# The recurrent gates of a hybrid layer in four matmuls per channel tile instead of six, with high and low input stacked on the partition halves

## The chip, the cores and the metric

The kernel runs on one core of one Trainium2 chip. The metric is the device time in microseconds of one execution. The matmul engine is called PE, the vector engine DVE, the scalar engine ACT, GpSimd POOL; SP issues most DMAs.

## The reference, cut to what matters

Two layers over 1024 tokens of width 2048. Each has one combined projection of the normalised input; a sliding-window attention; and a recurrent part of 1024 channels, whose two gates (r and i) come from 16 blocks of 64 channels with 64x64 weights each. Everything is float32.

```python
for l in range(DEPTH):
    h = _rmsnorm(x, norm_gain[l])
    proj = jnp.einsum('bsd,de->bse', h, w_in[l])
    q, k, v, g_attn, x_rnn, g_rnn = jnp.split(proj, splits, axis=-1)
    attn = _swa_sink_attention(q, k, v, sinks[l], cos, sin)
    xc = _causal_conv(x_rnn, conv_w[l], conv_b[l])
    rnn = _rg_lru(xc, w_rgate[l], b_rgate[l], w_igate[l], b_igate[l], lru_param[l])
    mixed = jnp.concatenate([attn * jax.nn.silu(g_attn), rnn * jax.nn.silu(g_rnn)], axis=-1)
    x = x + jnp.einsum('bse,ed->bsd', mixed, w_out[l])
...
xb = xc.reshape(b, s, N_RNN_BLOCKS, RNN_BLOCK)
r = jax.nn.sigmoid(jnp.einsum('bshi,hij->bshj', xb, w_r).reshape(b, s, D_RNN) + b_r)
i = jax.nn.sigmoid(jnp.einsum('bshi,hij->bshj', xb, w_i).reshape(b, s, D_RNN) + b_i)
log_a = -LRU_C * r.astype(jnp.float32) * jax.nn.softplus(-lru_param.astype(jnp.float32))
a = jnp.exp(log_a)
mult = jnp.sqrt(-jnp.expm1(2.0 * log_a))
u = mult * (i * xc).astype(jnp.float32)
_, h = lax.associative_scan(_lin_combine, (a, u), axis=1)
```

## The kernel before

Tokens lie along the free dimension, channels on the 128 partitions. The sequence is done in two halves of 512 tokens (`h`), each through both layers (`l`), so a layer is passed four times. A pass is cut into 200 slots (`s`). In each slot PE does one unit of the large projections: 12 matmuls of 128x512 into `proj`, each tile's product being three matmuls, because a float32 operand is split into a high and a low part in a rounded format (`F32R`): high by high, high by low, low by high.

Every unit's weights (`wraw`) come by DMA four slots ahead; ACT rounds them to the high part (`weight_hi`, L471) and DVE subtracts for the low part (`weight_lo`, L774) three slots before PE needs them. ACT may round the weights of slot s + 3 only when PE has finished unit s - 1, so ACT's and DVE's work of slot s begins as PE begins unit s.

All other work is written by hand into these slots, and each engine runs its own instructions strictly in program order, with semaphores between the engines. Two lists place what matters here:

- The attention goes in 16 visits b at the slots `VISIT[b]` = 31, 35, 39, 44, 48, 53, 57, 61, 66, 70, 75, 79, 83, 88, 92, 97 (then 101, 105). PE does scores (L400), transposes of the probabilities (`prob_transposes`, L413, in slot `VISIT[b+1]+1`) and values (L421). The transposes of visit b wait until ACT has copied the result of visit b-1 out of the same PSUM bank (`attn_out`, L593, in the same slot of ACT's program). ACT's exponents are L577 and L579, its copy of the transposed probabilities L587.
- The recurrent channels go in 8 tiles j of 128 channels at the slots `R0[j]` = 48, 54, 64, 70, 80, 86, 96, 102. With S for `R0[j]`: in slot S DVE takes the projection out and starts the convolution (L922 to L936, done in S+1), ACT and DVE split the gate weights `gw` into `gwcut` (L602, L942). In S+2 ACT rounds the convolved tile `xc` (`conv_hi`, L609) and DVE subtracts (`conv_lo`, L948) into `xcut`. In S+3 PE computes the r gate of all 128 channels, in S+4 the i gate, each with three 128x512 matmuls (`gate`, L438) into the one PSUM bank `ps_g`; the 128x128 weights are two 64x64 blocks on the diagonal and zeros. ACT reads r out with a tanh in S+4 (`rnn_r`, L615) and i in S+5 (`rnn_i`, L622), into `r_in` and `i_in`, the two halves of `sqr`. Then follow `lru_z` on DVE (S+5), `rnn_a` on ACT (S+6), `lru_m2` (S+7), `rnn_mult` on ACT with a table load (L639, S+7), and in S+9 on DVE `lru_scan` (L969, L970), which reads `i_in`. `gate_tanh` (L569) belongs to the output gates.

Since `R0` advances by 6 slots from an even to an odd tile and by 10 from an odd to an even one, slot S+4 of an odd tile is the slot after the scan of the tile before.

Of the kernel before, what the change touches and what calls it, by code (L numbers as in the profile page):

```python
# [7 lines left out]
F32 = mybir.dt.float32  # L8
# [5 lines left out]
P = 128  # L14
# [5 lines left out]
HD = 64  # L20
# [78 lines left out]
def build(nc, xt, w, gates, par, fgain, cossin, ident, out):  # L99
    with ExitStack() as ctx:  # L100
# [26 lines left out]
        acc = sb("acc", [TOK])  # L127
        gw = sb("gw", [GRING, 2, HD])
        gwcut = sb("gwcut", [2, 2, P], F32R)
# [126 lines left out]
        def _(sp_):  # L256
# [17 lines left out]
            for h in range(HALVES):  # L274
                for l in range(DEPTH):
                    for s in range(SLOTS):
# [22 lines left out]
                        if s + 8 in R0:  # L299
                            j = R0.index(s + 8)  # L300
                            n = l * RT + j

                            sp_.wait_ge(gw_lo, h * (2 * DEPTH * RT) + (2 * n + 2))
                            sp_.dma_start(gw[:, n % GRING, :, :], gates[l, j]).then_inc(gw_in[n % GRING], 16)
# [12 lines left out]
        @block.gpsimd  # L317
        def _(pool):
            pool.memset(gwcut[:, :, :, :].bitcast(F32), 0.0).then_inc(pool_set, 1)
# [3 lines left out]
            pool.wait_ge(pool_set, 4)  # L323

        @block.tensor
        def _(pe):
# [28 lines left out]
            def sum_of_squares(h, n):  # L355

                pe.wait_ge(acc_done, at_acc(h, KT * (n + 1)))
                if h == 0 and n == 0:
                    pe.wait_ge(par_in, 32)
                    pe.wait_ge(pool_set, 4)  # L360
# [63 lines left out]

            def gate(h, l, j, which):

                n = l * RT + j
                if which == 0:
# [36 lines left out]
        def _(act):  # L465
# [192 lines left out]
            act.activation(sp[:, 1, :, :], sp[:, 0, :, :], ACT.Exp, scale=-1.0).then_inc(abs_done, 1)  # L658
            act.wait_ge(pool_set, 4)
            act.wait_ge(par_in, 32)  # L660
            for h in range(HALVES):
                for l in range(DEPTH):
                    for s in range(SLOTS):
# [41 lines left out]
                        if s - 4 in R0:  # L705
                            rnn_r(h, l, R0.index(s - 4))
                        if s - 1 in G0:
# [8 lines left out]
                        for j in range(RT):  # L716
                            if s == R0[j] + 7:
                                rnn_mult(h, l, j)
                            if s == R0[j]:
                                gate_weights_hi(h, l, j)  # L720
                            if s == R0[j] + 5:
                                rnn_i(h, l, j)
                            if s == R0[j] + 6:
                                rnn_a(h, l, j)
# [28 lines left out]
        def _(dve):  # L753
            dve.sem_inc(evac, 4)
            dve.sem_inc(q_done, 1)
            dve.sem_inc(gw_lo, 2 * GRING)
            dve.memset(eps[:, :], EPS).then_inc(dve_set, 1)
# [180 lines left out]
            def gate_weights_lo(h, l, j):  # L938
                n = l * RT + j
                dve.wait_ge(gw_hi, h * (2 * DEPTH * RT) + (2 * n + 2))  # L940
                for a in (0, HD):
                    dve.tensor_tensor(gwcut[a:a + HD, 1, :, a:a + HD], gw[a:a + HD, n % GRING, :, :],  # L942
                                      gwcut[a:a + HD, 0, :, a:a + HD].bitcast(F32),
                                      ALU.subtract).then_inc(gw_lo, 1)

            def conv_lo(h, l, j):
                dve.wait_ge(xc_hi, per_layer(h, l, RT, j + 1))
                dve.tensor_tensor(xcut[:, 1, :], xc[:, :], xcut[:, 0, :].bitcast(F32),  # L948
                                  ALU.subtract).then_inc(xc_lo, 1)

            def lru_z(h, l, j):

                dve.wait_ge(r_done, per_layer(h, l, RT, j + 1))
                dve.tensor_scalar(r_in, r_in, 1.0, decay4[:, l, j:j + 1], ALU.add, ALU.mult).then_inc(z_done, 1)

            def lru_input(h, l, j):

                dve.wait_ge(i_done, per_layer(h, l, RT, j + 1))
                mark(dve.scalar_tensor_tensor(i_in, i_in, 1.0, xc[:, :], ALU.add, ALU.mult))
# [49 lines left out]
            for u in (2, 3):  # L1009
                weight_lo(u)  # L1010
            dve.wait_ge(pool_set, 4)
            for h in range(HALVES):
# [139 lines left out]
```

## Time and profile before

| | |
|---|---|
| median of 3 runs | 2394.43 us (2394.32 to 2394.78) |
| profiled execution | 2394.46 us |
| span of its instructions | 2392.6 us |
| PE busy | 2361.0 us, 99% of the span |
| DVE busy | 1399.6 us, 58% |
| ACT busy | 1194.5 us, 50% |
| DMA engines busy | about 33% |
| PE's granted clock, mean | 0.997 |

The span runs from the first to the last instruction on the core; the profiled execution took 1.9 us more than its span, and lies with the other runs. Busy times say how long an engine worked in all, not whether its work was on the path that sets the end.

### The profile page before, as it was taken

How to read it: one execution, taken by the hardware profiler on the slowest of the kernel's cores; microseconds unless marked ns; L12 is line 12 of the kernel's file. 1: busy time of each engine (PE TensorE's matmuls, PEld its weight loads, DVE VectorE, ACT ScalarE, POOL GpSimd, SP SyncE). 2: the span in 40 equal slices, each digit the busy share in tenths (PEclk: the TensorE clock that was granted, in tenths of full speed). 3: DMA queues.
4: the chain of work that ended last, by engine and by line, in shares of the span. 5: the costliest groups of instructions: out<-in, count | busy, mean ns of one | idle time of the engine just before them, and what ended most of it. 6: DMA issues, size and time to landing. Idle time of an engine off the chain costs nothing. (4 is left out here: it accounts for less than half of the span.)

```text
span 2392.6 us, 31126 instructions
## 1 busy us (share of the span) xinstructions
PE 2361.0 (99%) x11380; PEld 1904.4 (80%) x11380; DVE 1399.6 (58%) x2447; ACT 1194.5 (50%) x2357; POOL 1.2 (0%) x8
## 2 busy tenths in 40 slices
PE   8999999999999999999999999999999999999996
PEld 6877778888887777888888777788888777788885
DVE  7567765534546776544476677654354567756334
ACT  6556663324455665434455666542244566654332
POOL 0000000000000000000000000000000000000000
PEclk9999999999999999999999999999999999999998
DMA  5324223333332222353334432333333322233332
GB/s 183 98 82 158 87 80 98 97 98 96 96 94 82 83 80 86 97 167 94 98 116 128 159 102 81 88 97 97 97 98 93 94 80 82 81 88 97 97 97 105
DMA packets 126297, 241.28 MB, mean 101 GB/s; under 512 B 14144, under 2 KB 18496, under 8 KB 125376
## 3 DMA queue, kind: packets, MB, share of 16 engines
q1 hardware_dynamic: 125136, 237.03, 32.7%
q8 instruction: 89, 1.46, 0.2%
q10 hardware_dynamic: 1008, 2.26, 0.2%
q14 instruction: 64, 0.52, 0.1%
HBM read 230.85 MB, written 8.39 MB: 100 GB/s over the span
## 5 line engine op out<-in xcount | busy, mean ns | idle before, releaser
L351 PE MATMUL proj<-operand,wcut 128*128 128x512 f32 x9600 | 2227.4, 391 | 7.7 <-DVE wcut L774 6.4
L351 PEld LDWEIGHTS proj<-operand,wcut 128*128 128x128 f32 x9600 | 1794.3, 188 | 393.0 <-issue 19.2
L774 DVE TENSOR_TENSOR wcut<-wraw,wcut 128x512 fp32r<-128x512 f32 x800 | 552.2, 690 | 911.8 <-ACT wcut L471 908.8
L471 ACT ACTIVATE wcut<-wraw 128x512 fp32r<-128x512 f32 x800 | 504.3, 630 | 986.8 <-PE proj L351 975.4
L579 ACT ACTIVATE prob<-ps_sc,stat 128x128 f32<-128x128 f32 x256 | 89.9, 368 | 0.1
L549 ACT ACTIVATE gy<-proj 32x512 f32<-32x512 f32 x144 | 84.9, 589 | 3.8
L511 ACT ACTIVATE sqr<-x 128x512 f32<-128x512 f32 x64 | 38.0, 635 | 56.7 <-DVE x L979 56.6
L438 PE MATMUL ps_g<-xcut,gwcut 128*128 128x512 f32 x192 | 57.5, 408 | 0.0
L803 DVE TENSOR_TENSOR acc<-acc,sqr 128x512 f32<-128x512 f32 x78 | 53.9, 691 | 4.7
L639 ACT ACT_TABLE_LOAD x32 | 41.1, 1283 | 27.4 <-DVE mu L964 27.1
L579 ACT ACTIVATION_READ_ACCUMULATOR prob<-ps_sc,stat 128x1 f32 x256 | 53.4, 209 | 0.0
L934 DVE SCALAR_TENSOR_TENSOR xc<-xr,pars,xc 128x512 f32<-128x512 f32 x64 | 48.1, 752 | 2.1
L979 DVE TENSOR_TENSOR x<-proj,x 128x512 f32<-128x512 f32 x64 | 41.2, 685 | 11.6 <-PE proj L351 10.7
L569 ACT ACTIVATE gt<-gy 128x512 f32<-128x512 f32 x64 | 40.4, 632 | 14.2 <-DVE gy L883 12.7
L400 PEld LDWEIGHTS ps_sc<-kboth,q 64*64 64x64 f32 x1024 | 27.2, 132 | 24.4 <-issue 24.4
L915 DVE TENSOR_TENSOR prob<-prob,stat 128x512 f32<-128x512 f32 x64 | 44.3, 692 | 2.2
L895 DVE TENSOR_TENSOR mixed<-mixed,gy 128x512 f32<-128x512 f32 x64 | 44.3, 692 | 2.1
L905 DVE TENSOR_REDUCE stat<-ps_sc 128x4 f32<-128x512 f32 x64 | 44.2, 690 | 2.0
L878 DVE TENSOR_TENSOR gy<-proj,rstd 128x512 f32<-128x512 f32 x64 | 44.2, 690 | 1.9
L785 DVE TENSOR_TENSOR operand<-mixed,operand 128x512 fp32r<-128x512 f32 x64 | 41.7, 688 | 5.3 <-ACT operand L493 4.5
L883 DVE SCALAR_TENSOR_TENSOR gy<-gt,gy 128x512 f32<-128x512 f32 x64 | 43.9, 685 | 0.8
L413 PE MATMUL ps_t<-idn,prob 128*128 128x128 f32 x256 | 38.5, 273 | 4.8 <-ACT mixed L593 4.8
(108 smaller groups left out, 1100.7 us busy)
## 6 DMA issues: line engine op xcount, KB each, us to landing
wraw<-in_w SPq DMA_DIRECT2D x800, 256.0 KB, 2.6
x<-in_xt SPq DMA_DIRECT2D x2, 4096.0 KB, 13.3
mixed<-in_xt SPq DMA_DIRECT2D x14, 512.0 KB, 8.4
out<-x SPq DMA_DIRECT2D x4, 1024.0 KB, 4.7
tab<-in_cossin SPq DMA_DIRECT2D x8, 256.0 KB, 3.4
gw<-in_gates SPq DMA_DIRECT2D x32, 64.0 KB, 2.5
out<-x ACTq DMA_DIRECT2D x4, 512.0 KB, 2.9
out<-x SPq DMA_DIRECT2D x3, 512.0 KB, 2.9
```

What stands on the lines that cost most here:

```text
L351: last = pe.matmul(bank[:, :], wcut[:, u % RING, a, c:c + P], operand[:, k, b, :], start=(k == 0 and n == 0), stop=(k == KT - 1 and n == 2))
L438: last = pe.matmul(ps_g[:, :], gwcut[:, a, which, :], xcut[:, b, :], start=i == 0, stop=i == 2)
L471: act.activation(wcut[:, u % RING, 0, :], wraw[:, u % RING, :], ACT.Copy).then_inc(w_hi, 1)
L549: act.activation(gy[dst:dst + 32, 1, :], bank_of(l, tile)[src:src + 32, :], ACT.Copy).then_inc(shift_done, 1)
L579: act.activation(prob[:, t, :], ps_s[:, t // 2, t % 2, :], ACT.Exp, scale=HD ** -0.5, bias=stat[:, 1, t:t + 1], accum_out=stat[:, 3, t:t + ...
L774: dve.tensor_tensor(wcut[:, u % RING, 1, :], wraw[:, u % RING, :], wcut[:, u % RING, 0, :].bitcast(F32), ALU.subtract).then_inc(w_lo, 1)
L803: ins = dve.tensor_tensor(acc[:, :], acc[:, :], sqr[:, k % 2, :], ALU.add)
L878: dve.tensor_tensor(gy[:, n % 2, :], bank_of(l, tile)[:, :], rstd[:, :], ALU.mult).then_inc(evac, 1)
L895: dve.tensor_tensor(mixed[:, k, :], mixed[:, k, :], gy[:, n % 2, :], ALU.mult).then_inc(mixed_done, 1)
L905: mark(dve.tensor_reduce(stat[:, 0, :].rearrange("p (o a) -> p o a", o=2), ps_s, AX_X, ALU.max))
L915: dve.tensor_tensor(prob[:, :, :], prob[:, :, :], stat[:, 3, :].unsqueeze(2).to_broadcast([P, TPK, P]), ALU.mult).then_inc(p_done, 1)
L934: mark(dve.scalar_tensor_tensor(xc[:, :], src, wc, xc[:, :], ALU.mult, ALU.add))
```

## The change

The product of one tile is arranged anew. The unit is now one block of 64 channels (`part` 0 or 1) with both its gates, where it was one gate of both blocks. The contraction over 128 partitions holds the high part of the block's 64 inputs on one half and their low part on the other; the weights, repeated on both halves, hold r's and i's 64 columns side by side. So one matmul gives the high weights times high and low input, a second the low weights times both: two matmuls per block, four per tile.

```diff
-        gw = sb("gw", [GRING, 2, HD])
+        gw = sb("gw", [GRING, 2, P])
...
-            def gate(h, l, j, which):
+            def gate(h, l, j, part):
...
-                    pe.wait_ge(xc_lo, per_layer(h, l, RT, j + 1))
-                    pe.wait_ge(gw_lo, h * (2 * DEPTH * RT) + (2 * n + 2 + 2 * GRING))
+                    pe.wait_ge(xc_lo, per_layer(h, l, 2 * RT, 2 * j + 2))
+                    pe.wait_ge(gw_lo, h * (DEPTH * RT) + (n + 1 + GRING))
                     if j > 0:
-                        pe.wait_ge(i_done, per_layer(h, l, RT, j))
+                        pe.wait_ge(i_done, per_layer(h, l, 2 * RT, 2 * j))
                 else:
-                    pe.wait_ge(r_done, per_layer(h, l, RT, j + 1))
-                for i, (a, b) in enumerate(((0, 0), (0, 1), (1, 0))):
-                    last = pe.matmul(ps_g[:, :], gwcut[:, a, which, :], xcut[:, b, :],
-                                     start=i == 0, stop=i == 2)
+                    pe.wait_ge(i_done, per_layer(h, l, 2 * RT, 2 * j + 1))
+                for a in range(2):
+                    last = pe.matmul(ps_g[:, :], gwcut[:, part, a, :], xcut[:, part, :], start=a == 0, stop=a == 1)
...
-                for a in (0, HD):
-                    act.activation(gwcut[a:a + HD, 0, :, a:a + HD], gw[a:a + HD, n % GRING, :, :],
-                                   ACT.Copy).then_inc(gw_hi, 1)
+                act.activation(gwcut[:, :, 0, :], gw[:, n % GRING, :, :], ACT.Copy).then_inc(gw_hi, 1)
...
-                act.activation(xcut[:, 0, :], xc[:, :], ACT.Copy).then_inc(xc_hi, 1)
-            def rnn_r(h, l, j):
-                act.wait_ge(g_done, per_layer(h, l, 2 * RT, 2 * j + 1) + 2 * GRING)
-                if j > 0:
+                for part in range(2):
+                    rows = slice(HD * part, HD * part + HD)
+                    act.activation(xcut[rows, part, :], xc[rows, :], ACT.Copy).then_inc(xc_hi, 1)
+            def gate_out(h, l, j, part):
+                act.wait_ge(g_done, per_layer(h, l, 2 * RT, 2 * j + part + 1) + 2 * GRING)
+                if j > 0 and part == 0:
                     act.wait_ge(m2_done, per_layer(h, l, RT, j))
-                act.activation(r_in, ps_g[:, :], ACT.Tanh, scale=0.5,
-                               bias=pars[:, l, C_BR + j:C_BR + j + 1]).then_inc(r_done, 1)
-            def rnn_i(h, l, j):
-                act.wait_ge(g_done, per_layer(h, l, 2 * RT, 2 * j + 2) + 2 * GRING)
-                if j > 0:
                     act.wait_ge(scan_done, per_layer(h, l, RT, j))
-                act.activation(i_in, ps_g[:, :], ACT.Tanh, scale=0.5,
-                               bias=pars[:, l, C_BI + j:C_BI + j + 1]).then_inc(i_done, 1)
+                a, b = HD * part, HD * (1 - part)
+                act.activation(r_in[a:a + HD, :], ps_g[a:a + HD, :], ACT.Tanh, scale=0.5,
+                               bias=pars[a:a + HD, l, C_BR + j:C_BR + j + 1]).then_inc(r_done, 1)
+                act.activation(i_in[a:a + HD, :], ps_g[b:b + HD, :], ACT.Tanh, scale=0.5,
+                               bias=pars[b:b + HD, l, C_BI + j:C_BI + j + 1]).then_inc(i_done, 1)
...
             def conv_lo(h, l, j):
-                dve.wait_ge(xc_hi, per_layer(h, l, RT, j + 1))
-                dve.tensor_tensor(xcut[:, 1, :], xc[:, :], xcut[:, 0, :].bitcast(F32),
-                                  ALU.subtract).then_inc(xc_lo, 1)
+                for part in range(2):
+                    a, b = HD * part, HD * (1 - part)
+                    dve.wait_ge(xc_hi, per_layer(h, l, 2 * RT, 2 * j + part + 1))
+                    dve.tensor_tensor(xcut[b:b + HD, part, :], xc[a:a + HD, :],
+                                      xcut[a:a + HD, part, :].bitcast(F32), ALU.subtract).then_inc(xc_lo, 1)
...
-                dve.wait_ge(r_done, per_layer(h, l, RT, j + 1))
+                dve.wait_ge(r_done, per_layer(h, l, 2 * RT, 2 * j + 2))
```

The slots stay as they were: `gate_out(.., 0)` stands where `rnn_r` stood (S+4), `gate_out(.., 1)` where `rnn_i` stood (S+5). DVE's split of the gate weights becomes one operation over 128 partitions instead of two over 64, the gates' DMA carries 128 KB instead of 64 KB, and one memset at the start is gone. The rest of the diff renumbers waits and lays out weights and biases on the host.

On ACT, around tile 3 of a pass, from the rounding of its input to its gates' read-out, this stood before (names in brackets are the semaphores waited for; the numbers behind `w_in` are buffers):

```order
L609 ACTIVATE xcut<-xc 128x512 [waits g_done,conv_done,w_hi]
L587 ACTIVATE probT<-ps_t 128x512 [waits v_done,t_done]
L577 ACT_TABLE_LOAD [waits t_done]
L577 ACTIVATE stat<-stat 128x4 [waits max_done]
L579 ACTIVATE prob,stat<-ps_sc,stat 128x128 x4
L471 ACTIVATE wcut<-wraw 128x512 [waits unit_done,w_in0]
L569 ACTIVATE gt<-gy 128x512 [waits gate_done,evac,w_hi]
L471 ACTIVATE wcut<-wraw 128x512 [waits unit_done,w_in1]
L615 ACTIVATE sqr<-ps_g,pars 128x512 [waits m2_done,g_done,w_hi]
L471 ACTIVATE wcut<-wraw 128x512 [waits unit_done,w_in2]
L569 ACTIVATE gt<-gy 128x512 [waits gate_done,evac,w_hi]
L622 ACTIVATE sqr<-ps_g,pars 128x512 [waits scan_done,g_done]
```

and this stands there now, from the same place on (lines are those of the changed kernel):

```order
L607 ACTIVATE xcut<-xc 64x512 [waits g_done,conv_done,w_hi]
L607 ACTIVATE xcut<-xc 64x512
L585 ACTIVATE probT<-ps_t 128x512 [waits v_done,t_done]
...
L469 ACTIVATE wcut<-wraw 128x512 [waits unit_done,w_in1]
L616 ACTIVATE sqr<-ps_g,pars 64x512 [waits m2_done,scan_done,g_done,w_hi]
L618 ACTIVATE sqr<-ps_g,pars 64x512
L469 ACTIVATE wcut<-wraw 128x512 [waits unit_done,w_in2]
L567 ACTIVATE gt<-gy 128x512 [waits gate_done,evac,w_hi]
L616 ACTIVATE sqr<-ps_g,pars 64x512 [waits g_done]
L618 ACTIVATE sqr<-ps_g,pars 64x512
```

Each single operation on 128 partitions has become two on 64, and the wait for the scan (`scan_done`) has moved from the second read-out to the first, one slot earlier.

On PE, at the same tile, before:

```order
L438 MATMUL ps_g<-xcut,gwcut 128x512 [waits i_done,gw_lo,xc_lo]
L438 MATMUL ps_g<-xcut,gwcut 128x512 x2
L351 MATMUL proj<-operand,wcut 128x512 [waits w_lo]
L351 MATMUL proj<-operand,wcut 128x512 x11
L438 MATMUL ps_g<-xcut,gwcut 128x512 [waits r_done]
L438 MATMUL ps_g<-xcut,gwcut 128x512 x2
```

and now:

```order
L437 MATMUL ps_g<-xcut,gwcut 128x512 [waits i_done,gw_lo,xc_lo]
L437 MATMUL ps_g<-xcut,gwcut 128x512
L350 MATMUL proj<-operand,wcut 128x512 [waits w_lo]
L350 MATMUL proj<-operand,wcut 128x512 x11
L437 MATMUL ps_g<-xcut,gwcut 128x512 [waits i_done]
L437 MATMUL ps_g<-xcut,gwcut 128x512
```

One matmul is gone from each group, and the second group, which waited for the r read-out, waits for both read-outs of the first block; one unit of 12 matmuls still lies between the groups.

## Rows read from the trace of the kernel before

**Rows 1.** Windows of the whole run: PE busy (count), granted clock; first column the stretch

```profile
6.40:10.40 4.00, 4.00 (x10) 3.13 (x11) 2.46 (x4) 2.62 (x6) 0.00 (x0) 1.00 1.02 378
40.00:2370.00 2330.00, 2324.31 (x11237) 1876.17 (x11237) 1358.27 (x2384) 1161.74 (x2303) 0.00 (x0) 1.00 0.33 98
2373.00:2379.20 6.20, 1.98 (x4) 0.67 (x4) 3.40 (x2) 3.91 (x6) 0.00 (x0) 1.00 0.00 0
2379.30:2392.60 13.30, 0.00 (x0) 0.00 (x0) 9.57 (x16) 0.00 (x0) 0.00 (x0) 0.50 0.80 315
```

**Rows 2.** Timeline, PE, the first tile's gates: start us, length us, operation

```profile
162.21 0.85 PE L438 MATMUL ps_g<-xcut,gwcut 128*128 128x512 f32 x3
...
162.90 2.91 PE L351 MATMUL proj<-operand,wcut 128*128 128x512 f32 x12
```

**Rows 3.** Groups by shape, whole run: busy us, mean ns of one

```profile
L615 ACT ACTIVATE sqr<-ps_g,pars 128x512 f32<-128x512 f32 x32 | 22.1, 689 | 17.9 <-PE ps_g L438 11.3 <-issue 4.2 <-ACT wcut L471 2.0
...
L609 ACT ACTIVATE xcut<-xc 128x512 fp32r<-128x512 f32 x32 | 20.3, 633 | 30.2 <-DVE xc L936 25.6 <-ACT wcut L471 2.9 <-issue 1.3
...
L942 DVE TENSOR_TENSOR gwcut<-gw,gwcut 64x128 fp32r<-64x128 f32 x64 | 18.2, 284 | 1.4
```

**Rows 4.** Timeline, tile 3 of the second layer, first half

```profile
821.72 0.63 ACT L609 ACTIVATE xcut<-xc 128x512 fp32r<-128x512 f32 x1 [0.98 <-ACT wcut L471]
822.26 0.58 ACT L587 ACTIVATE probT<-ps_t 128x512 f32<-128x512 f32 x1
...
826.30 0.69 DVE L774 TENSOR_TENSOR wcut<-wraw,wcut 128x512 fp32r<-128x512 f32 x1 [2.74 <-ACT wcut L471]
...
827.49 0.69 ACT L615 ACTIVATE sqr<-ps_g,pars 128x512 f32<-128x512 f32 x1
...
828.56 0.85 PE L438 MATMUL ps_g<-xcut,gwcut 128*128 128x512 f32 x3
828.77 1.28 DVE L970 TENSOR_TENSOR_SCAN mixed<-acc,hlast,sqr 128x512 f32<-128x512 f32 x1
```

**Rows 5.** Timeline, tile 1 of the same layer

```profile
772.54 1.28 DVE L970 TENSOR_TENSOR_SCAN mixed<-acc,hlast,sqr 128x512 f32<-128x512 f32 x1
...
774.20 0.37 ACT L593 ACTIVATE mixed<-ps_t 128x256 f32<-128x256 f32 x1
...
776.10 0.60 PE L413 MATMUL ps_t<-idn,prob 128*128 128x128 f32 x4
...
780.98 0.69 DVE L774 TENSOR_TENSOR wcut<-wraw,wcut 128x512 fp32r<-128x512 f32 x1 [2.00 <-ACT wcut L471]
...
788.01 0.39 ACT L593 ACTIVATE mixed<-ps_t 128x256 f32<-128x256 f32 x1
...
789.55 0.60 PE L413 MATMUL ps_t<-idn,prob 128*128 128x128 f32 x4
```

**Rows 6.** Timeline, tiles 4 and 5 of the same layer

```profile
866.48 0.63 ACT L471 ACTIVATE wcut<-wraw 128x512 fp32r<-128x512 f32 x1 [0.53 <-PE proj L351]
...
877.29 1.28 ACT L569 ACT_TABLE_LOAD   x1 [0.33 <-issue]
...
879.12 0.36 ACT L593 ACTIVATE mixed<-ps_t 128x256 f32<-128x256 f32 x1
...
879.63 0.63 PE L413 MATMUL ps_t<-idn,prob 128*128 128x128 f32 x4 [0.95 <-ACT mixed L593]
...
880.38 1.28 DVE L970 TENSOR_TENSOR_SCAN mixed<-acc,hlast,sqr 128x512 f32<-128x512 f32 x1
...
883.53 0.85 PE L438 MATMUL ps_g<-xcut,gwcut 128*128 128x512 f32 x3
```

**Rows 7.** Timeline, tile 6 of the same layer

```profile
908.68 0.63 ACT L609 ACTIVATE xcut<-xc 128x512 fp32r<-128x512 f32 x1 [2.59 <-DVE xc L936]
909.22 0.36 ACT L593 ACTIVATE mixed<-ps_t 128x256 f32<-128x256 f32 x1
...
909.73 0.63 PE L413 MATMUL ps_t<-idn,prob 128*128 128x128 f32 x4 [0.24 <-ACT mixed L593]
```

More of the change, by code:

```diff
@@ L301, in _ @@
                             n = l * RT + j
-                            sp_.wait_ge(gw_lo, h * (2 * DEPTH * RT) + (2 * n + 2))
+                            sp_.wait_ge(gw_lo, h * (DEPTH * RT) + (n + 1))
                             sp_.dma_start(gw[:, n % GRING, :, :], gates[l, j]).then_inc(gw_in[n % GRING], 16)
@@ L318, in _ @@
         def _(pool):
-            pool.memset(gwcut[:, :, :, :].bitcast(F32), 0.0).then_inc(pool_set, 1)
             pool.memset(ones[:, :], 1.0).then_inc(pool_set, 1)
@@ L322, in _ @@
             pool.memset(vhist[:, :, :], 0.0).then_inc(pool_set, 1)
-            pool.wait_ge(pool_set, 4)
+            pool.wait_ge(pool_set, 3)
         @block.tensor
@@ L359, in sum_of_squares @@
                     pe.wait_ge(par_in, 32)
-                    pe.wait_ge(pool_set, 4)
+                    pe.wait_ge(pool_set, 3)
                 if n:
@@ L423, in values @@
                 last.then_inc(v_done, 1)
-            def gate(h, l, j, which):
+            def gate(h, l, j, part):
                 n = l * RT + j
-                if which == 0:
-                    pe.wait_ge(xc_lo, per_layer(h, l, RT, j + 1))
-                    pe.wait_ge(gw_lo, h * (2 * DEPTH * RT) + (2 * n + 2 + 2 * GRING))
+                if part == 0:
+                    pe.wait_ge(xc_lo, per_layer(h, l, 2 * RT, 2 * j + 2))
+                    pe.wait_ge(gw_lo, h * (DEPTH * RT) + (n + 1 + GRING))
                     if j > 0:
-                        pe.wait_ge(i_done, per_layer(h, l, RT, j))
+                        pe.wait_ge(i_done, per_layer(h, l, 2 * RT, 2 * j))
                 else:
-                    pe.wait_ge(r_done, per_layer(h, l, RT, j + 1))
-                for i, (a, b) in enumerate(((0, 0), (0, 1), (1, 0))):
-                    last = pe.matmul(ps_g[:, :], gwcut[:, a, which, :], xcut[:, b, :],
-                                     start=i == 0, stop=i == 2)
+                    pe.wait_ge(i_done, per_layer(h, l, 2 * RT, 2 * j + 1))
+                for a in range(2):
+                    last = pe.matmul(ps_g[:, :], gwcut[:, part, a, :], xcut[:, part, :], start=a == 0, stop=a == 1)
                 last.then_inc(g_done, 1)
@@ L658, in _ @@
             act.activation(sp[:, 1, :, :], sp[:, 0, :, :], ACT.Exp, scale=-1.0).then_inc(abs_done, 1)
-            act.wait_ge(pool_set, 4)
+            act.wait_ge(pool_set, 3)
             act.wait_ge(par_in, 32)
@@ L705, in _ @@
                         if s - 4 in R0:
-                            rnn_r(h, l, R0.index(s - 4))
+                            gate_out(h, l, R0.index(s - 4), 0)
                         if s - 1 in G0:
@@ L721, in _ @@
                             if s == R0[j] + 5:
-                                rnn_i(h, l, j)
+                                gate_out(h, l, j, 1)
                             if s == R0[j] + 6:
@@ L755, in _ @@
             dve.sem_inc(q_done, 1)
-            dve.sem_inc(gw_lo, 2 * GRING)
+            dve.sem_inc(gw_lo, GRING)
             dve.memset(eps[:, :], EPS).then_inc(dve_set, 1)
@@ L939, in gate_weights_lo @@
                 n = l * RT + j
[L940 to L944, printed above, removed]
-            def conv_lo(h, l, j):
-                dve.wait_ge(xc_hi, per_layer(h, l, RT, j + 1))
-                dve.tensor_tensor(xcut[:, 1, :], xc[:, :], xcut[:, 0, :].bitcast(F32),
-                                  ALU.subtract).then_inc(xc_lo, 1)
+                dve.wait_ge(gw_hi, h * (DEPTH * RT) + (n + 1))
+                dve.tensor_tensor(gwcut[:, :, 1, :], gw[:, n % GRING, :, :], gwcut[:, :, 0, :].bitcast(F32),
+                                  ALU.subtract).then_inc(gw_lo, 1)
+            def conv_lo(h, l, j):
+                for part in range(2):
[3 more added lines that the diff above has]
+                                      xcut[a:a + HD, part, :].bitcast(F32), ALU.subtract).then_inc(xc_lo, 1)
             def lru_z(h, l, j):
-                dve.wait_ge(r_done, per_layer(h, l, RT, j + 1))
+                dve.wait_ge(r_done, per_layer(h, l, 2 * RT, 2 * j + 2))
                 dve.tensor_scalar(r_in, r_in, 1.0, decay4[:, l, j:j + 1], ALU.add, ALU.mult).then_inc(z_done, 1)
             def lru_input(h, l, j):
-                dve.wait_ge(i_done, per_layer(h, l, RT, j + 1))
+                dve.wait_ge(i_done, per_layer(h, l, 2 * RT, 2 * j + 2))
                 mark(dve.scalar_tensor_tensor(i_in, i_in, 1.0, xc[:, :], ALU.add, ALU.mult))
@@ L1010, in _ @@
                 weight_lo(u)
-            dve.wait_ge(pool_set, 4)
+            dve.wait_ge(pool_set, 3)
             for h in range(HALVES):
@@ L1129 @@
     wo = arr(w_out).reshape(DEPTH, UPG, KU, P, OG, GW).transpose(0, 4, 1, 3, 2, 5)
-    first = {"q": 0, "kv": 4, "ga": 5, "xr": 9, "gr": 13, "o": PG}
-    source = [first[GROUPS[g][0]] + GROUPS[g][1] for g, _ in STREAM]
+    start = {"q": 0, "kv": 4, "ga": 5, "xr": 9, "gr": 13, "o": PG}
+    source = [start[GROUPS[g][0]] + GROUPS[g][1] for g, _ in STREAM]
     w = np.concatenate([wi, wo], axis=1)[:, source, [j for _, j in STREAM]]
     w = w.reshape(DEPTH, SLOTS, P, KU * GW)
-    gates = np.stack([arr(w_rgate), arr(w_igate)], axis=3).reshape(DEPTH, RT, P, 2, HD)
+    wr, wg = (arr(a).reshape(DEPTH, RT, 2, HD, HD) for a in (w_rgate, w_igate))
+    first = np.concatenate([wr[:, :, 0], wg[:, :, 0]], axis=3)
+    second = np.concatenate([wg[:, :, 1], wr[:, :, 1]], axis=3)
+    gates = np.tile(np.stack([first, second], axis=3), (1, 1, 2, 1, 1))
     sink = arr(sinks).reshape(DEPTH, NKV, 2, 2, 2).transpose(3, 0, 1, 4, 2).reshape(2, DEPTH, AT)
@@ L1138 @@
     cw = tiles(conv_w).transpose(0, 1, 3, 2).reshape(P, DEPTH, RT * CW)
-    par = np.concatenate([tiles(norm_gain), sink, cw, tiles(conv_b), tiles(b_rgate), tiles(b_igate),
+    bi = np.roll(tiles(b_igate), HD, axis=0)
+    par = np.concatenate([tiles(norm_gain), sink, cw, tiles(conv_b), tiles(b_rgate), bi,
                           tiles(lru_param)], axis=2)
```

## The prediction

> **What bounds the kernel now.** I read the windows first: between 40 and 2370 us PE is busy 2324.31 of 2330.00 us at the full granted clock, DVE and ACT about half the time [rows 1]. So PE's queue sets the time: a matmul removed counts in full, and so does every wait inserted. Then I read the timeline around the gates for the price of one matmul: three begin at 162.21 and the unit behind them at 162.90, so one takes 0.23 us [rows 2], not the 0.85 that the row shows from first start to last end. Last I went, tile by tile, to the instruction that releases PE behind each gate, to see how much earlier than PE it was ready. That is the reading that decides here: ACT and DVE have room on average, but each runs in order, and PE's waits on them sit at a few fixed places.
>
> **What the change removes.** 2 of 6 matmuls in each of 32 tiles: 64 x 0.23 = 14.7 us, 3.68 us for each of the four passes through a layer. PE has nothing else to do then, so all of it counts if nothing else is late. The new matmuls have the same shape and should cost the same. The memset and the larger gates DMA cost nothing: the memset's engine is idle, and the weights are asked for eight slots ahead of their use.
>
> **What it adds.** No row shows these operations on 64 partitions. Below, a half-width operation could cost half; above, as much as the full one: 633 ns for the rounding, 689 for the tanh [rows 3]. The nearest row is DVE's split of the gate weights on 64 partitions, 284 ns for 128 elements a partition [rows 3]: 0.41 of the tanh's time for a quarter of its length, which is no sign of a discount for half the partitions. I take the full durations. Two in a row overlap a little: from one start to the next 0.54 us on ACT [rows 4], and about 0.59 for the tanh. So ACT gets 0.54 in S+2 and 0.59 in each of S+4 and S+5; DVE gets 0.6 for the second subtraction, and saves some 0.17 on the gate weights (two operations of 284 against one of twice the row length; between 0 and 0.3). That is 55 us more work on ACT in all, hidden behind PE's units except where PE is released by it. Four places are left.
>
> *Tile 3.* This is the large term. The first read-out now writes half of `i_in` too, so it waits for the scan of tile 2, which reads `i_in`. In the trace the r read-out began at 827.49, and that scan ran from 828.77 to 830.05 [rows 4]. The chain that leads to the scan starts at the rounding at 821.72; the second rounding puts 0.54 in front of the exponents, DVE waits 2.74 us for what follows them (826.30), and 0.17 is saved before: the scan ends 0.37 later, at 830.42. Then 0.04 to start, 0.59 + 0.69 for the two tanh, and 0.15 until PE goes on (an ACT result at 879.48 released PE at 879.63 [rows 6]): 831.89. PE arrives at its second group at 828.56 less the matmul saved in the first, 828.33. It stands for **3.56 us**. Queued behind are unit 75 and all of PE's program, so it counts in full. Bounds: with roundings and tanh at half price 2.7, with no overlap and nothing saved on DVE 3.9. The other three passes have the same order.
>
> *Tile 1.* The scan of tile 0 ended at 773.82 [rows 5]; the second subtraction stands right before it on DVE, so 774.42. The two tanh take ACT to 775.64, and behind them in its queue is `attn_out` (0.37 us), for which PE's transposes wait: 776.01 + 0.15 = 776.16, where PE would be at 776.10 - 0.23 = 775.87. That is 0.29. In the next slots DVE's delay of 0.6 passes to ACT and the second block's extra tanh adds 0.59; DVE was already waiting 2.00 us for ACT at 780.98 [rows 5], so all of it, some 1.15, reaches the `attn_out` that ended at 788.40. PE's transposes then start at 789.70, with PE there at 789.55 - 0.46 + 0.29 = 789.38: 0.32. Together **0.61**; bounds 0 and 1.2.
>
> *Tiles 4 and 5.* Before tile 5's gates PE already waits 0.95 us for ACT [rows 6]. What is saved on tile 4 (0.46) only lengthens that wait, unless ACT is early too. ACT had 0.53 of idle time at 866.48 for the extra tanh, which leaves its chain some 0.2 early; the second rounding adds 0.54, against 0.33 idle at 877.29. The transposes then start where they did: the 0.46 is lost. The scan of tile 4 ends at 881.66 - 0.2 + 0.6 = 882.06, so PE is released at 882.06 + 0.04 + 0.59 + 0.69 + 0.15 = 883.53, and would be there at 883.30: 0.23. Together **0.69**; bounds 0.3 and 1.3.
>
> *Tile 6.* PE waits 0.24 for `attn_out`, which follows the rounding directly [rows 7]. The second rounding, less the 0.17, delays it by **0.37**; bounds 0 and 0.6.
>
> Elsewhere the read-outs end a microsecond or more before PE needs them.
>
> **The sum.** Per pass: -3.68 + 3.56 + 0.61 + 0.69 + 0.37 = +1.55. Four passes: +6.2 us. The profiled execution took 2394.46 us, 0.03 off the median, so 2394.46 + 6.2 = **2400.7 us**. The bounds of the four places add up to 3.0 and 7.0 a pass, which gives 4 x (-3.68 + 3.0) = -2.7 to 4 x (-3.68 + 7.0) = +13.3: 2391.7 to 2407.7. The likeliest case's own range is 2397 to 2405.
>
> **Rivals.**
> - *The clock falls in the waits.* At the end of the run PE's last work ended at about 2375, the granted clock was still 1.00 until 2379.2, and 0.50 after 2379.3 [rows 1]. [...] If it falls, the units behind run slow until the clock is given back. At the start of the run PE's first 4.00 us held 10 matmuls [rows 1], where 17 fit at 0.23: 1.7 us lost. Four falls: 2400.7 + 6.8 = 2407.5, more if the clock stays low longer. Against it: the wait is shorter than the one that is known to have dropped it. [...]
> - *Only the large wait is real.* The small ones rest on sums of tenths. If slack swallows them, each pass is -3.68 + 3.56: 2394.0, no change. For it: most of them are 0.2 to 0.4 us. Against: at 879.63 and 909.73 PE waits for ACT already, and there any delay counts.
> - *The saving wins.* The scan of tile 2 comes early enough. It decides from a wait of about 2.4 us: with 0.9 us less in front of the scan, or half-width tanh and roundings much cheaper than full ones. If tile 3 had but its second tanh to wait for (r ended 0.38 before PE's 828.56 [rows 4]), its wait would be 0.2 to 0.4, and the sum -3.68 + 0.3 + 1.67 = -1.7 a pass: 2387.6; with no waits at all 2379.8. Against: `scan_done` is waited for by name, and its time is read from the trace.
>
> **How the numbers follow.** A difference of 0.2%, 4.8 us, is about what a measurement of this kernel can tell from no change. I give the forecast 0.47, the clock 0.18, only the large wait 0.24, the saving 0.11. Slower by over 0.2% means above 2399.2: about two thirds of the forecast's 2397 to 2405 and all of the clock's, with a tail of the forecast's beyond.  Slower 0.54, within 0.2% 0.35, faster 0.11. The range goes from the lower bound of the sum (2392) to the clock's case with something over (2409), which leaves out the saving's 2387.6 and below.
>
> **What would show it.** Right: ps_g's matmuls number 128 and are 0.23 apart; in the list of PE's waits a new row, second gate group on ACT's tanh, four times 3.3 to 3.9 us and four times about 0.2; the transposes (L413 before) wait more than 4.8 us in all, some 9; the first read-out of tile 3 starts 0.05 after the scan's end; ACT's 64-partition tanh lasts about 690 ns; the granted clock stays at 1.00 between first and last unit. Wrong: a half-width tanh near 350 ns; the scan of tile 2 ending before PE's first group; waits of PE for weights (`wcut`), since ACT stands blocked for some 3 us at tile 3 with the rounding of unit 78's weights behind it (four slots of room, so I cost it at nothing; gone, it would cost the excess over 8 us); or a clock of 0.50 behind a wait.

## The result, and the profile after

The changed kernel takes 2421.73 us (median of four runs, 2420.25 to 2423.5) against 2394.59 beside it (2394.32 to 2394.78): 27.1 us more, ratio 1.0114, interval 1.0098 to 1.013. The predicted time was 2400.7. Direction and largest term came out, the size did not. The profiled execution took 2422.28 us, 27.8 more than that of before.

The page of the changed kernel (busy, share of the span, count; then groups: busy, mean ns of one | idle before, releaser):

```profile
PE 2361.0 (98%) x11316; PEld 1899.2 (78%) x11316; DVE 1418.2 (59%) x2447; ACT 1258.5 (52%) x2421; POOL 0.7 (0%) x7
...
L616 ACT ACTIVATE sqr<-ps_g,pars 64x512 f32<-64x512 f32 x64 | 43.8, 684 | 36.4 <-DVE mixed L966 27.0 <-PE ps_g L437 8.2
L437 PE MATMUL ps_g<-xcut,gwcut 128*128 128x512 f32 x128 | 44.8, 432 | 15.2 <-ACT sqr L618 15.2
...
L607 ACT ACTIVATE xcut<-xc 64x512 fp32r<-64x512 f32 x64 | 40.4, 631 | 27.1 <-DVE xc L932 23.1
...
L944 DVE TENSOR_TENSOR xcut<-xc,xcut 64x512 fp32r<-64x512 f32 x64 | 43.9, 686 | 2.8 <-ACT xcut L607 0.9
```

Half the partitions bring no discount at all: the tanh takes 684 ns on 64 partitions against 689 on 128, the rounding 631 against 633 [rows 3]. PE's busy time stands at 2361.0 as before, although 64 matmuls are gone. That is the first sign that some of its matmuls ran slower. The waits show how long PE stood (total us, times, longest):

```profile
PE ps_t L412 <- ACT mixed L591: 18.0, 16, 2.0
PE ps_g L437 <- ACT sqr L618: 15.2, 7, 3.6
PE proj L350 <- DVE wcut L770: 6.5, 1, 6.5
```

The second row is the forecast's new wait, four times 3.6 us and three times 0.23. The first was forecast at some 9 us and is twice that. The third, at the start of the run, was there before.

The timeline of tile 3, second layer, first half (start us, length us), answers to [rows 4]:

```profile
831.91 0.62 PE L437 MATMUL ps_g<-xcut,gwcut 128*128 128x512 f32 x2
...
832.37 2.92 PE L350 MATMUL proj<-operand,wcut 128*128 128x512 f32 x12
...
836.06 1.28 DVE L966 TENSOR_TENSOR_SCAN mixed<-acc,hlast,sqr 128x512 f32<-128x512 f32 x1
...
837.46 0.68 ACT L616 ACTIVATE sqr<-ps_g,pars 64x512 f32<-64x512 f32 x1 [2.71 <-DVE mixed L966]
...
838.17 0.68 ACT L618 ACTIVATE sqr<-ps_g,pars 64x512 f32<-64x512 f32 x1
...
838.91 1.22 PE L437 MATMUL ps_g<-xcut,gwcut 128*128 128x512 f32 x2 [3.62 <-ACT sqr L618]
```

The first read-out stands until the scan of tile 2 is done, then the two tanh start 0.71 us apart, and PE follows. Unforecast are the 1.22 us of the last row: the same two matmuls took 0.62 at 831.91. The windows of the low clock, between the first and the last unit, say why (stretch, its length, PE busy and count; behind the other engines the granted clock, then DMA share and GB/s; last their sum). The granted clock reads 0.50 in each of them, and 1.00 in all other time between those two units:

```profile
244.41:247.82 3.41, 3.41 (x10) 2.53 (x8) 1.05 (x2) 1.36 (x2) 0.00 (x0) 0.50 0.38 115
838.33:841.74 3.41, 2.83 (x7) 2.25 (x8) 2.91 (x5) 3.15 (x5) 0.00 (x0) 0.50 0.27 77
892.94:896.36 3.42, 3.42 (x10) 2.67 (x9) 3.31 (x6) 1.90 (x3) 0.00 (x0) 0.50 0.12 40
1435.66:1442.49 6.83, 5.33 (x13) 4.17 (x14) 3.79 (x7) 3.99 (x6) 0.00 (x0) 0.50 0.33 98
2032.99:2039.82 6.83, 5.99 (x14) 4.46 (x14) 3.14 (x6) 3.39 (x6) 0.00 (x0) 0.50 0.33 96
sum 23.90, PE 20.98 PEld 16.09 DVE 14.21 ACT 13.79 POOL 0.00; mean PE 4.20 PEld 3.22 DVE 2.84 ACT 2.76 POOL 0.00
```

Four of the five go with tile 3's wait, one in each pass; 892.94 follows a wait of 1.98 us before tile 5's gates. At 838.33, 1435.66 and 2032.99 it fell while PE still stood; at 244.41 and 892.94 it fell 1.3 and 1.2 us after PE had gone on. In all, PE worked 21.0 us at a granted clock of 0.50. The pair's 1.22 us against 0.62 put work there at twice its time, so the cost is estimated at up to half of the 21.0.

### The profile page after: what moved, and what is told of

It reads as the page before. It is cut to its first block and busy times, and to the rows that moved or that the text cites. A ratio compares the mean times of both kernels' runs of the same rounds, so it can differ in the third digit from the quotient of the medians.

```text
span 2420.5 us, 31069 instructions
## 1 busy us (share of the span) xinstructions
PE 2361.0 (98%) x11316; PEld 1899.2 (78%) x11316; DVE 1418.2 (59%) x2447; ACT 1258.5 (52%) x2421; POOL 0.7 (0%) x7
## 5 line engine op out<-in xcount | busy, mean ns | idle before, releaser
L616 ACT ACTIVATE sqr<-ps_g,pars 64x512 f32<-64x512 f32 x64 | 43.8, 684 | 36.4 <-DVE mixed L966 27.0
L437 PE MATMUL ps_g<-xcut,gwcut 128*128 128x512 f32 x128 | 44.8, 432 | 15.2 <-ACT sqr L618 15.2
L607 ACT ACTIVATE xcut<-xc 64x512 fp32r<-64x512 f32 x64 | 40.4, 631 | 27.1 <-DVE xc L932 23.1
L412 PEld LDWEIGHTS ps_t<-idn,prob 128*128 128x128 f32 x256 | 30.5, 139 | 30.5 <-issue 24.3
L944 DVE TENSOR_TENSOR xcut<-xc,xcut 64x512 fp32r<-64x512 f32 x64 | 43.9, 686 | 2.8 <-ACT xcut L607 0.9
## 6 DMA issues: line engine op xcount, KB each, us to landing
x<-in_xt SPq DMA_DIRECT2D x2, 4096.0 KB, 13.6
```

What stands on the lines that cost most here:

```text
L412: last = pe.transpose(ps_t[:, t, :], prob[:, t, :], idn[:, :])
L437: last = pe.matmul(ps_g[:, :], gwcut[:, part, a, :], xcut[:, part, :], start=a == 0, stop=a == 1)
```

## The experiments

Three questions: what the large wait costs and whether the clock belongs to it; why the small waits are twice what was forecast; and what the four matmuls are worth without the waits. "Before" and "changed" name the kernel an edit was made in. All times stand beside 2394.5 to 2394.6 for the kernel before.

### The scan's wait alone, in before

```diff
+                    act.wait_ge(scan_done, per_layer(h, l, RT, j))   # in rnn_r
...
-                    act.wait_ge(scan_done, per_layer(h, l, RT, j))   # in rnn_i
```

> The kernel before, with nothing moved but the wait for the scan: it stands at the r read-out (slot S+4) instead of the i read-out (S+5). Theory (a wait counts in full, and the clock falls only in a longer stand): at tile 3 the r read-out starts after 830.05 instead of at 827.49, so PE's second gate group starts at 830.05 + 0.04 + 0.69 + 0.15 = 830.93 instead of 828.56: 2.37 us a pass, 9.5 us in all, about 2404 us; tiles 1 and 5 have room for it; clock at 1.00 throughout. Rival (any stand of a few us drops the clock): the same waits and low-clock stretches behind them, 1.7 to 3.4 us more for each, 2411 to 2418 us. Rival (the wait is hidden): 2395 us.

2408.1 us, ratio 1.0056 (1.0039 to 1.0073). Its waits, PE's timeline at tile 3, and windows behind it:

```profile
PE ps_g L438 <- ACT sqr L616: 8.8, 4, 2.2
```

```profile
829.37 2.90 PE L351 MATMUL proj<-operand,wcut 128*128 128x512 f32 x12
834.47 0.97 PE L438 MATMUL ps_g<-xcut,gwcut 128*128 128x512 f32 x3 [2.20 <-ACT sqr L616]
835.28 4.51 PE L351 MATMUL proj<-operand,wcut 128*128 128x512 f32 x12
```

```profile
835.32:838.73 3.41, 3.41 (x10) 2.64 (x9) 2.18 (x4) 1.21 (x2) 0.00 (x0) 0.50 0.49 106
838.75:842.00 3.25, 3.25 (x30) 2.06 (x29) 1.39 (x3) 2.06 (x5) 0.00 (x0) 1.00 0.21 73
```

A unit that lasts 2.90 us before the wait lasts 4.51 behind it. By the units' start times the wait costs 2.47 us a pass, 9.9 in all; the remaining 3.7 are the clock's. It fell behind three of the four waits, though each was the same 2.2 us. So both theories hold half: the wait as worked out, and the clock on top.

### Only the halves, in before

Rounding, subtraction and both read-outs each as two operations on 64 partitions; matmuls and waits as before. Shown for the rounding, the rest likewise:

```diff
-                act.activation(xcut[:, 0, :], xc[:, :], ACT.Copy).then_inc(xc_hi, 1)
+                for a in (0, HD):
+                    act.activation(xcut[a:a + HD, 0, :], xc[a:a + HD, :], ACT.Copy).then_inc(xc_hi, 1)
```

> The kernel before, with its six matmuls and their order, but the rounding, the subtraction and both read-outs of a tile done in two operations of 64 partitions each instead of one of 128. Theory (two operations on different partition halves do not overlap at all, so a pair costs 0.66 more on ACT for the rounding and 0.71 for a tanh, and the delay is handed on from tile 5 to tile 6): PE waits 1.1 at tile 3, 0.5 more at tile 5's transposes, some 1.3 more at tile 6's: 2.9 a pass, 11.7 in all, about 2406 us. Rival (they overlap as the prediction had it, 0.54 and 0.59, and nothing is handed on): 0.75 + 0.2 + 0.54 a pass, about 2400.6 us. Rival (half as many partitions take half the time): 2395 us.

2408.74 us, ratio 1.0059 (1.0044 to 1.0074).

```profile
PE ps_t L413 <- ACT mixed L593: 13.2, 12, 1.8
...
PE ps_g L438 <- ACT sqr L617: 4.1, 4, 1.0
```

The small waits come from the halves alone, and they are larger than forecast even without the large wait: +14.2 us. By the units' start times in the third pass they cost 0.69 us at tile 1, 1.28 at tile 3, 0.81 at tile 5 and 0.79 at tile 6. The theory's 1.3 at tile 6 did not come: DVE lies 10.4 us later than before there, and so does PE, so nothing is handed on. No clock is in this number:

```profile
40.00:2385.00 2345.00, 2326.82 (x11241) 1876.32 (x11240) 1381.29 (x2417) 1231.66 (x2400) 0.00 (x0) 1.00 0.33 97
```

### The halves, one kind at a time, in before

First the rounding and the subtraction alone, then the read-outs alone, with the edit above cut to these.

> The kernel before, with only the rounding and the subtraction of a tile's input in two operations of 64 partitions; read-outs and matmuls as before. Theory (a pair does not overlap: 0.66 on ACT): PE waits 0.43 at tile 3, 0.33 more at tile 5's transposes, 0.66 more at tile 6's: 1.4 a pass, about 2400.2 us. Rival (what costs is the read-outs): 2396 us or less.

> The kernel before, with only the two read-outs in two operations of 64 partitions each; rounding, subtraction and matmuls as before. Theory (0.71 more in S+4 and in S+5, handed on along ACT's and DVE's queues): 0.5 at tile 3, 0.2 at tile 5's transposes, 0.7 handed on to tile 6's, 0.3 at tile 1's second transposes: 1.7 a pass, about 2401 us; tile 6's transposes wait longer though nothing in front of them changed since the end of tile 5. Rival (tile 6's wait comes from its own rounding alone, nothing is handed on): 0.24 there as before, 2398.5 us.

2402.01 us (ratio 1.0031, 1.0019 to 1.0043) and 2398.1 us (ratio 1.0015, 1.0005 to 1.0024). PE's waits, first kernel:

```profile
PE ps_t L413 <- ACT mixed L593: 10.1, 8, 1.7
...
PE ps_g L438 <- ACT sqr L616: 1.3, 4, 0.3
```

and second:

```profile
PE ps_t L413 <- ACT mixed L593: 6.1, 8, 1.3
PE ps_g L438 <- ACT sqr L616: 0.9, 4, 0.2
```

The roundings cost 7.5 us, the read-outs 3.5: together 11.0, where both at once cost 14.2. So 3.2 us exist only together. In the second kernel tile 6's wait stayed at 0.24, which fits the rival of its expectation: alone, the read-outs of tile 5 hand nothing on to tile 6. Both at once leave 0.53 at tile 1's later transposes, which neither does alone; most of the 3.2 us are there (0.69 a pass by start times), the rest at tile 3.

### Two matmuls per gate, in before

The third product of each gate is left out, so the gates lack it; nothing else changes.

```diff
-                for i, (a, b) in enumerate(((0, 0), (0, 1), (1, 0))):
+                for i, (a, b) in enumerate(((0, 0), (0, 1))):
```

> The kernel before, with the third matmul of each gate (low weights by high input) left out, so the gates are computed from the high part of the weights alone. Everything else is as before. It measures the saving of 64 matmuls by itself. Theory: 64 x 0.23 = 14.7 us less, of which some 1 us is lost at tile 5's transposes, where PE waits for ACT anyway: about 2381 us. Rival (the saving is smaller than its share of PE's time, since PE's other waits swallow it): 2388 us or more.

2380.86 us, ratio 0.9943 (0.9928 to 0.9958). 13.65 us for 64 matmuls are 0.213 each, not 0.23. The waits at the transposes stayed at 0.95 and 0.24, and the saving counted all the same. That the theory's 2381 was met is luck: it took a larger saving less 1 us of loss, and there was no loss. The prediction's step that what is saved on tile 4 only lengthens tile 5's wait does not hold here: ACT's chain starts from PE's units and came as much earlier.

### The large wait filled, in the changed kernel

Thirteen matmuls of zero weights go into the bank of the unit in progress ahead of the wait at tile 3; they add nothing to its sum. The zeros are set once at the start.

```diff
+                    if j == 3:
+                        g = STREAM[R0[j] + 4][0]
+                        bank = proj[2 * ((l * (PG + OG) + g) % 2)]
+                        for _ in range(FILL):
+                            pe.matmul(bank[:, :], zero[:, :], operand[:, 0, 0, :], start=False, stop=False)
```

> The changed kernel, with 13 idle matmuls ahead of the wait at tile 3's second gate group: zero weights, accumulated into the bank in progress, so that they add nothing to the result. They fill 13 x 0.23 = 3.0 of the 3.8 us in which PE stands there, and take nothing away from the wait itself. Theory (part of the loss is the clock that falls behind this wait): the gap shrinks to some 0.8 us, the second group starts when it did, no low-clock stretch at tile 3, and the time falls by the clock's share of the loss, some 8.7 us by the low-clock stretches of the changed kernel: about 2413 us. Rival (the low clock in the record costs nothing, the waits are longer than counted): 2421 us, or more if the filling itself costs.

2414.38 us, ratio 1.0083 (1.0068 to 1.0098): 7.35 us under the changed kernel. PE's timeline, and windows before and behind the gate:

```profile
834.66 3.20 PE L442 MATMUL proj<-operand,zero 128*128 128x512 f32 x13
838.44 0.73 PE L445 MATMUL ps_g<-xcut,gwcut 128*128 128x512 f32 x2 [0.58 <-ACT sqr L626]
839.01 2.90 PE L353 MATMUL proj<-operand,wcut 128*128 128x512 f32 x12
```

```profile
834.70:838.40 3.70, 3.16 (x14) 2.22 (x12) 3.60 (x7) 1.37 (x2) 0.00 (x0) 1.00 0.25 71
838.44:842.00 3.56, 3.56 (x16) 2.71 (x18) 2.33 (x4) 2.60 (x4) 0.00 (x0) 1.00 0.40 97
1486.91:1490.32 3.41, 3.41 (x11) 2.83 (x12) 3.24 (x8) 1.13 (x3) 0.00 (x0) 0.50 0.24 77
```

From the unit ahead to the gate it is 6.54 us in both kernels (831.90 to 838.44; 832.37 to 838.91 in the changed kernel), so the gate was ready no sooner; but its two matmuls take 0.73 instead of 1.22 and the unit behind 2.90. The 7.35 us are therefore clock, and a lower bound for its price at tile 3: the third window is one of two falls that came behind the 1.98 us before tile 5, where the changed kernel has one.

### A buffer of its own for i of odd tiles, in the changed kernel

The read-out of tile j then waits for the scan of tile j-2.

```diff
+        def i_of(j):
+            return vfeat[:, 0:TOK] if j % 2 else i_in
...
-                    act.wait_ge(scan_done, per_layer(h, l, RT, j))
+                if j > 1 and part == 0:
+                    act.wait_ge(scan_done, per_layer(h, l, RT, j - 1))
```

> The changed kernel, with the i gate of odd tiles in a buffer that is free at that time, so that a tile's first read-out waits for the scan of the tile two before it, and never in fact. Nothing else differs. Theory (the wait for the scan makes PE stand long enough for the clock to fall): the scan's part of tile 3's wait goes, 1.4 of 3.8 us is left because ACT comes late; the first wait at tile 1 and the gate's at tile 5 go; no low-clock stretch; the waits that are left, about 3.7 us a pass, eat the saving of 3.68: about 2395 us. Rival (the loss is in the half-width operations and not in the wait for the scan): over 2410 us. Rival (the clock falls whatever the wait): low-clock stretches remain, over 2403 us.

2400.95 us, ratio 1.0026 (1.0015 to 1.0037): 20.8 us under the changed kernel, and 6 over what was expected.

```profile
PE ps_t L415 <- ACT mixed L594: 15.6, 12, 2.0
...
PE ps_g L440 <- ACT vfeat L622: 3.7, 4, 0.9
```

```profile
1505.98 0.63 PE L415 MATMUL ps_t<-idn,prob 128*128 128x128 f32 x4 [0.76 <-ACT mixed L594]
```

The large wait is down to 0.9, but the small ones keep 15.6 us, and behind two of the four waits of 1.97 to 1.98 us the clock fell. Of the 15.6, 4.8 stood there before the change; the other 10.8 and the 3.7 at tile 3 together outweigh the saving of 13.65. The last row is tile 6's wait in the third pass: 0.76, where the changed kernel has 1.75.

### Second block's work in other slots as well

On top of the kernel above, the second block's rounding and subtraction move to S+3, behind `attn_out`, and its read-out to the front of ACT's slot S+5. PE's first group then waits for the first block's subtraction alone.

```diff
+                        if s - 5 in R0:
+                            gate_out(h, l, R0.index(s - 5), 1)
...
+                        if s - 3 in R0:
+                            conv_hi(h, l, R0.index(s - 3), 1)
```

> The changed kernel with the i gate of odd tiles in its own buffer, and two things moved: the second block's rounding and subtraction one slot later (S+3, behind the copy of the attention's result), the second read-out to the front of slot S+5, ahead of the exponents. Theory (what is left of the loss is ACT's order at three places): tile 3 still waits about 1, tile 1's second transposes none, tile 5's 1.0 as before the change, tile 6's about 0.3; the rest of the saving of 13.6 comes through: about 2386 us, clock at 1.00 throughout. Rival (ACT and DVE simply have too much to do in these slots, so the waits only move): 2395 us or more.

2392.12 us, ratio 0.999 (0.9981 to 0.9999), 6 over what was expected.

```profile
PE ps_t L415 <- ACT mixed L595: 10.0, 8, 1.6
...
PE ps_g L441 <- ACT vfeat L622: 4.1, 4, 1.0
```

The second rounding no longer stands before `attn_out`, yet the transposes still wait, 0.89 at tile 1 and 1.6 at tile 5. What else stands ahead of `attn_out` in ACT's slot is the next suspect.

### The attention copy at the front of ACT's slot

Twice: on top of the last kernel (with tile 1's `rnn_mult` one slot later, and tile 3's first read-out ahead of `weight_hi`), and alone in before.

```diff
+                        for b in range(NB):
+                            if s == VISIT[b + 2] + 1:
+                                attn_out(h, l, b)
```

> The version with its own i buffer and the moved slots, and three more things moved on ACT: the copy of the attention's result (for which PE's transposes wait) to the front of its slot, tile 1's root with its table load one slot later, and tile 3's first read-out ahead of the rounding of weights in its slot. Theory (all of the loss was the order of ACT's work in front of three waits of PE, not its amount): the transposes wait for nothing, also not the 0.95 and 0.24 of before the change; tile 3 waits some 0.5 at most; the 13.6 us of the saving and the 6 of the old waits come through: about 2377 us. Rival (the amount of ACT's work binds in these slots): no better than 2388 us.

> The kernel before, with the copy of the attention's result at the front of its slot on ACT, and nothing else changed. It says how much of the last version's time has nothing to do with the gates. Theory: the eight waits of PE's transposes (0.95 and 0.24 in each pass, 1.1 and 0.4 by the start times) go: 6 us less, about 2388.5 us. Rival (they only move to the read-outs behind the copy): 2393 us or more.

2379.79 us (2379.56 to 2380.08), ratio 0.9939 (0.9925 to 0.9952), and 2388.26 us, ratio 0.9973 (0.9963 to 0.9983). In both the transposes wait for nothing. All that is left of the changed gates' waits in the first, and its window:

```profile
PE ps_g L441 <- ACT vfeat L622: 3.5, 8, 0.5
```

```profile
40.00:2360.00 2320.00, 2314.87 (x11184) 1866.02 (x11182) 1377.47 (x2386) 1225.07 (x2370) 0.00 (x0) 1.00 0.34 99
```

Between the two lies the worth of the four matmuls once ACT's order suits them: 2388.26 - 2379.79 = 8.5 us. The 13.65 of the matmuls less the 3.5 of waits would be 10.2. Most of the difference is that a wait costs more than its row says: by start times, against the second kernel, PE loses 0.52 us at tile 3's second gate group and 0.70 at tile 5's in each pass, 4.9 in all, which leaves 8.8. The last 0.3 us are not accounted for.

## Why the prediction was wrong

**PE as the bound, and the saving.** Right. Every wait and every matmul counted in full; a matmul is worth 0.213 us, which makes the saving 13.65 instead of 14.7.

**Durations of the halves.** Right: full price, 684 and 631 ns; DVE's split of the gate weights takes 0.42 where two took 0.57 [rows 3].

**Tile 3.** Right in place, mechanism and nearly in size: by start times 3.78 us a pass against 3.56. The scan's wait alone gives 2.47 there (first experiment), the halves alone 1.28 (second).

**Spacing of the halves.** The first step that failed: the overlap of [rows 4], 0.54 from one start to the next, was carried to pairs that start on different partition halves. The timeline of the changed kernel at tile 1:

```profile
774.39 1.29 ACT L607 ACTIVATE xcut<-xc 64x512 fp32r<-64x512 f32 x2
...
776.85 1.40 DVE L944 TENSOR_TENSOR xcut<-xc,xcut 64x512 fp32r<-64x512 f32 x2
```

Two roundings of 0.63 take 1.29, two subtractions of 0.69 take 1.40: no overlap. The tanh pair starts 0.71 apart. The operation behind a pair does not overlap either: in the third pass the next rounding of weights starts 1.32 us after the pair's first (1486.90 and 1488.22), where it started 0.54 after the single rounding before the change. So to what stands behind it a second rounding costs 0.77 instead of 0.54, a second tanh 0.84 instead of 0.59, a second subtraction 0.84 instead of 0.6. On DVE too the next subtraction (`weight_lo`) starts 1.43 us after the pair's first in the third pass (1488.36 and 1489.79), where it started 0.60 after the single one before (1469.14 and 1469.74). What decides it was tried on neither engine.

**The small waits.** Terms of the sum mis-sized, by the units' start times in the third pass, in us a pass:

| place | predicted | measured |
|---|---|---|
| tile 1 | 0.61 | 1.45 |
| tile 3 | 3.56 | 3.78 |
| tiles 4 and 5 | 0.69 | 1.55 |
| tile 6 | 0.37 | 1.50 |

With the saving at 3.68, as the terms were read with 0.23 a matmul, this is +4.60 instead of +1.55; with all four passes like the third, +18.4 instead of +6.2. Tile 6 shows the kind of error that weighs most. It was taken as fed afresh by PE, so that only its own second rounding counted. ACT and then PE in the third pass of the changed kernel:

```profile
1493.83 0.69 ACT L616 ACTIVATE sqr<-ps_g,pars 64x512 f32<-64x512 f32 x1 [2.25 <-DVE mixed L966]
...
1506.20 0.63 ACT L635 ACTIVATE mu<-mu 128x512 f32<-128x512 f32 x1 [1.37 <-DVE mu L960]
...
1517.07 0.63 ACT L469 ACTIVATE wcut<-wraw 128x512 fp32r<-128x512 f32 x1 [2.11 <-PE proj L350]
1521.01 1.28 ACT L607 ACTIVATE xcut<-xc 64x512 fp32r<-64x512 f32 x2 [3.31 <-DVE xc L932]
1522.32 0.39 ACT L591 ACTIVATE mixed<-ps_t 128x256 f32<-128x256 f32 x1
```

```profile
1518.06 3.04 PE L350 MATMUL proj<-operand,wcut 128*128 128x512 f32 x12
1522.84 0.63 PE L412 MATMUL ps_t<-idn,prob 128*128 128x128 f32 x4 [1.75 <-ACT mixed L591]
```

DVE's convolution of tile 6, in before and in the changed kernel:

```profile
1499.86 0.75 DVE L936 SCALAR_TENSOR_TENSOR xc<-xr,pars,xc 128x512 f32<-128x512 f32 x1
```

```profile
1520.18 0.75 DVE L932 SCALAR_TENSOR_TENSOR xc<-xr,pars,xc 128x512 f32<-128x512 f32 x1
```

Against before's trace PE lies 19.6 us later here. At tile 5 ACT stands 2.25 us for the scan of tile 4, and with the second block's two tanh behind that, its rounding of weights at 1500.11 comes 20.9 us later. That passes to DVE (`lru_z` and `weight_lo` wait for ACT), and over `lru_m2` back to ACT's `rnn_mult`, the second row. By 1511.63 ACT has caught up: three roundings of weights wait for PE again (0.20, 1.61 and 2.11 us) and lie 19.6 us later, as PE does. But DVE's queue keeps 20.6, and 20.3 after the shorter split of the gate weights, and tile 6's rounding waits for DVE. So 0.7 us are handed on from tile 5 over some 25 us of program, although ACT is half idle, and the second rounding adds 0.77: together the 1.50. ACT's 3.31 us of idle time before the rounding are no slack, since DVE's result ends them. The source is the wait for the scan at tile 5: with the buffer of its own, where it is gone, tile 6's wait is 0.76 instead of 1.75, and the halves in before hand nothing on.

**The clock.** The second step that failed: the fall of the clock was left out of the sum. The rival with 0.18 came true in kind; its time, 2407.5, did not, since it stood on the same small waits. Of the 27.8 us between the profiled executions, 18.4 are start times as above; 9.4 are left, of which filling the wait gave at least 7.35 back, and 21.0 us of PE's work at a granted 0.50 allow 10.5, if it takes twice as long there. The start times behind tile 3 show it directly. In the second pass its second gate group comes 10.35 us later than before (828.56 to 838.91) and the next values 11.53 later (832.08 to 843.61), though one matmul of 0.23 is saved between: 1.4 us for this fall. The four falls there cost 1.6, 1.4, 2.6 and 2.9 us, 8.5 in all. The fifth, behind tile 5, slowed its units by 1.2 us, but tile 6's wait in that pass shrank from 1.75 to 0.74, so it cost next to nothing:

```profile
923.53 0.63 PE L412 MATMUL ps_t<-idn,prob 128*128 128x128 f32 x4 [0.74 <-ACT mixed L591]
```

The rival's 1.7 was taken from a stretch whose granted clock reads 1.00 [rows 1], so no row of before showed that price. What spoke against the rival, that the wait is shorter than the one known to have dropped the clock (PE's last work in before ended at 2375.0, and the clock read 1.00 until 2379.2 [rows 1]), was no argument: here waits of 2.0 to 3.6 us dropped it. Behind tile 3 the clock was low in all four passes: in three of them from the first matmul behind the wait, so that the first two took 1.22 us, and in the first pass (244.41) only from 1.3 us behind it, where the first two took 0.73.

**Parts and whole.** The forecast was 21.0 us short: 12.2 in the waits (18.4 against 6.2) and most of the rest in the clock, which stood at nothing. The scan's wait alone gives +13.6, the halves +14.2, the matmuls -13.65: +14.2 together, where the change gives +27.1. Some 9 of the other 13.0 are waits: by start times in the third pass the two parts give 2.47 + 3.57 = 6.04 us, the changed kernel 8.28. The 2.24 between lie at tile 1 (0.76), tiles 4 and 5 (0.74) and tile 6 (0.71); at tile 3 the two simply add up. The changed kernel with a buffer of its own, where the scan's wait is gone, gives 1.42, 1.22, 1.07 and 0.54 at the four places. So at tile 6, and for the most part at tile 5, the surplus goes with the scan's wait, which alone costs PE nothing there. At tile 1 it does not, and what makes it was not tried. The rest, some 4, goes with the clock: 2.2 and 1.0 us of wait at tile 3 become 3.6, behind which it fell every time, and at tile 5 the wait grows from 1.76, behind which it never fell, to 1.98, behind which it sometimes does.

## What to carry to other kernels

Where two operations take the place of one, a shared buffer moves the wait for its last reader to the front of the pair; look up what is late there, and give the pair a buffer of its own. An engine half idle has no slack if its idle time ends on another engine that waited for it: follow the delay in both queues, since one may have caught up while the other still carries it. And price a new stop of TensorE of about two microseconds or more at the units behind it at half clock too, or fill it: of the 20 stops of 1.97 us or more between first and last unit in these profiles, 12 had a stretch at 0.50 behind them.

## What was not expected of the hardware

The granted clock and the stops of PE before it, over all profiles between first and last unit: after 3.6 us (changed kernel) it fell in 4 of 4 cases; after 2.2 (scan's wait alone) in 3 of 4; after 1.97 to 2.00 in 5 of 12 (changed kernel, filled wait, own buffer); after 1.76 (four times in the halves in before) or less in none. The same stop in the same program has both outcomes, so its length alone does not decide. Each fall shows 3.41 or 6.83 us at 0.50.

A matmul of 128x512 is worth 0.213 us when it is taken out of a group, though starts lie 0.23 apart [rows 2]; why was not settled.
